# Forgetting attention with weights scaled before they are turned, and an output made in turned form

## What is computed

```python
def forgetting_attention(q, k, v, log_f):
    F = cumsum(log_f, axis=1).transpose(0, 2, 1)
    for blk in range(T // 128):
        logits = einsum('bhqd,bhkd->bhqk', qh[:, :, q0:kend], kh[:, :, :kend])
        logits = logits + F[:, :, q0:kend, None] - F[:, :, None, :kend]
        logits = where(causal, logits, NEG_INF)
        p = softmax(logits, axis=-1)
        outs.append(einsum('bhqk,bhkd->bhqd', p, vh[:, :, :kend]))

h = h + concatenate([ret, fox], axis=-1) @ w_out
```

## Time and profile before

| | us |
|---|---|
| median of 3 runs | 913.65 |
| lowest, highest | 913.23, 914.32 |
| the profiled execution | 913.05 |
| its span, first to last instruction | 911.3 |
| TensorE busy | 898.2 |
| VectorE busy | 586.4 |
| ScalarE busy | 448.1 |
| GpSimd busy | 113.8 |

### The profile page before, as it was taken

The page is one execution under the profiler, slowest core; times in us unless marked ns, Lnnn a source line. Parts: engine busy times, 40 slices in busy tenths (PEclk is TensorE's granted clock), DMA queues, the critical chain, the costliest instruction groups (busy, mean ns, idle before and its releaser), DMA issues.

```text
span 911.3 us, 12621 instructions
## 1 busy us (share of the span) xinstructions
PE 898.2 (99%) x5039; PEld 766.6 (84%) x5039; DVE 586.4 (64%) x834; ACT 448.1 (49%) x632; POOL 113.8 (12%) x83
## 2 busy tenths in 40 slices
PE   9999999999999999999999999999999999999998
PEld 6887887888978999988888889888877888889886
DVE  5378988996686666644456647877765565554542
ACT  6265456854545555533344436645553544444431
POOL 0431225656110000000000002100100000000200
PEclk9999999999999999999999999999999999999999
DMA  8774542334235555555567535524540565554562
GB/s 285 201 247 141 184 139 93 133 112 125 83 104 175 185 185 183 183 188 185 185 203 280 186 94 186 185 93 139 185 138 29 169 203 187 186 173 148 190 216 69
DMA packets 83554, 149.74 MB, mean 164 GB/s; under 512 B 8480, under 2 KB 16208, under 8 KB 83376
## 3 DMA queue, kind: packets, MB, share of 16 engines
q1 hardware_dynamic: 80352, 144.55, 48.3%
q10 hardware_dynamic: 2528, 3.63, 1.1%
q0 software_dynamic: 624, 0.87, 0.8%
HBM read 147.59 MB, written 1.44 MB: 164 GB/s over the span
## 4 chain that ended last, share of the span: by engine, by line
PE 86%; DVE 8%; ACT 2%; DMA 2%; POOL 1%; issue 1%; DVEq 0%; SPq 0%; ACTq 0%; POOLq 0%
PE gemm L494 63%; PE mixbank L980 5%; PE gemm L980 5%; DMA raw<-in_w_in_dram 2%; PE mixbank L677 2%; DVE mix L1942 2%; PE mixbank L555 2%; PE mixbank L652 2%; DVE w_lo L1713 1%; PE mixbank L839 1%; PE mixbank L663 1%; ACT w_hi L1201 1%; POOL mix L2480 1%; PE gemm L566 1%; PE mixbank L1161 1%
## 5 line engine op out<-in xcount | busy, mean ns | idle before, releaser
L1713 DVE TENSOR_TENSOR w_lo<-raw,w_hi 128x2048 fp32r<-128x2048 f32 (+3 forms) x131 | 285.2, 2187 | 187.8 <-ACT w_hi L1201 187.6
L1201 ACT ACTIVATE w_hi<-raw 128x2048 fp32r<-128x2048 f32 (+3 forms) x140 | 255.3, 1833 | 173.2 <-DMA raw<-in_w_in_dram 50.0
L494 PE MATMUL gemm<-w_hi,s_hi 128*128 128x512 f32 (+3 forms) x784 | 208.7, 386 | 0.7 <-issue 0.4
L494 PE MATMUL gemm<-w_lo,s_hi 128*128 128x512 f32 (+3 forms) x784 | 201.7, 377 | 0.1
L494 PE MATMUL gemm<-w_hi,s_lo 128*128 128x512 f32 (+3 forms) x784 | 201.6, 377 | 0.0
L494 PEld LDWEIGHTS gemm<-w_lo,s_hi 128*128 128x128 f32 x784 | 142.7, 188 | 27.5 <-DVE w_lo L1713 0.3
L494 PEld LDWEIGHTS gemm<-w_hi,s_lo 128*128 128x128 f32 x784 | 142.7, 188 | 27.5
L494 PEld LDWEIGHTS gemm<-w_hi,s_hi 128*128 128x128 f32 x784 | 139.7, 188 | 27.4 <-issue 2.8
L2447 POOL TENSOR_TENSOR sm<-sm 128x2 f32<-128x2 f32 (+4 forms) x13 | 22.7, 1750 | 493.0 <-DVE sm L1757 313.2
L2441 POOL TENSOR_TENSOR w_lo<-raw,w_hi 128x2048 fp32r<-128x2048 f32 x9 | 41.3, 4602 | 158.5 <-ACT w_hi L1201 158.5
L1218 ACT ACTIVATE mix<-gemm,sm 128x512 f32<-128x512 f32 (+2 forms) x25 | 16.3, 654 | 60.9 <-PE gemm L494 60.9
(11 more groups left out here) (333 smaller groups left out, 1172.1 us busy)
## 6 DMA issues: line engine op xcount, KB each, us to landing
raw<-in_w_in_dram SPq DMA_DIRECT2D x40, 1024.0 KB, 5.0
raw<-in_w_mlp_up_dram SPq DMA_DIRECT2D x16, 1024.0 KB, 5.3
raw<-in_w_mlp_down_dram SPq DMA_DIRECT2D x16, 1024.0 KB, 5.0
raw<-in_w_gate_dram SPq DMA_DIRECT2D x10, 1024.0 KB, 5.0
raw<-in_w_up_dram SPq DMA_DIRECT2D x10, 1024.0 KB, 5.0
raw<-in_w_down_dram SPq DMA_DIRECT2D x10, 1024.0 KB, 5.0
raw<-in_w_out_dram SPq DMA_DIRECT2D x8, 1024.0 KB, 5.0
raw<-in_w_xkv_dram SPq DMA_DIRECT2D x8, 1024.0 KB, 5.1
```

The lines of the kernel that those rows point to most:

```text
L494: return nc.tensor.matmul(G[b % 2][t][:, 0:width], lhs, rhs, start=kt == 0 and not (low_x or low_w), stop=kt == blk["kt"] - 1 and (low_x i ...
L1201: nc.scalar.activation(w_hi[:, n % SLOTS, 0:kn, 0:width], raw[:, n % SLOTS, 0:kn, 0:width], ACT.Copy)\
L1713: V.tensor_tensor(w_lo[:, s, 0:kn, 0:width], raw[:, s, 0:kn, 0:width], w_hi[:, s, 0:kn, 0:width].bitcast(F32), ALU.subtract)\
```

## The change

- `scaled` on VectorE takes the place of `normed` for the forgetting attention: when the exponentials of a group are there it takes the reciprocal of the sums and multiplies the 128x512 weights in LM2 by it, in place, and then signals `att_norm`. It stands behind `greatest` of the next group and ahead of the copy of its own.
- TensorE's `turned` waits for `att_norm` there instead of `att_exp`.
- `weighed_features` takes the place of `weighed`: values are stationary (64 columns), turned weights move (128 columns). The output has features on partitions; even heads go to partitions 0 to 63, odd heads to 64 to 127 of M[3].
- ScalarE's `fox_out` copies M[3] to a new tile FOXT (in the half of MG2 that is no longer needed), and signals `out_copied`, for which the next `weighed_features` waits.
- The transposes of banks 2 and 3 of MG2 go; `s_hi` and `s_lo` of these are made from FOXT, and B_O2 runs without a break.
- `ret_oc` is renamed `out_copied`; ScalarE counts `turn_pe` by itself.

```diff
-                pe.wait_ge(sem("att_exp"), g + 1)
+                pe.wait_ge(sem("att_norm" if features_out else "att_exp"), g + 1)
...
+                def weighed_features(k):
+                    t, heads = work[k]
+                    g = g0 + k
+                    pe.wait_ge(sem("att_ptc"), g + 1)
+                    if k >= 1:
+                        pe.wait_ge(sem("out_copied"), NT + k)
+                    per = keys_of(work, k) // P
+                    for j, h in enumerate(heads):
+                        o = M[3][64 * (j % 2):64 * (j % 2) + 64, P * (j // 2):P * (j // 2) + P]
+                        for s in range(per):
+                            last = nc.tensor.matmul(o, values(h, s), exps_turned[:, g % 2, (j * per + s) * P:][:, 0:P], start=s == 0, stop=s == per - 1)
+                    last.then_inc(sem("att_out"), 1)
...
-            mm(B_O2, turned=24, quarters=[0])
-            turn(lambda kt, t: MG2[:, t, P * kt:P * kt + P], lambda q: [("att_norm", 12)], banks=range(2, 4))
-            mm(B_O2, turned=24, quarters=[1, 2, 3])
+            mm(B_O2, turned=24)
...
+            def fox_out(k):
+                t, heads = WORK_A[k]
+                n = len(heads) // 2
+                act.wait_ge(sem("att_out"), len(WORK_A) + k + 1)
+                dst = FOXT[:, heads[0] // 2:heads[0] // 2 + n, P * t:P * t + P]
+                nc.scalar.activation(dst, M[3][:, 0:P * n].rearrange("p (a b) -> p a b", a=n), ACT.Copy).then_inc(sem("out_copied"), 1)
...
             for k in attention(WORK_A, lambda t, h: 1.0, lambda g: LM2[:, g % 2], LM2):
                 if k < 2:
                     split(B_KV + 3, k)
...
                 if k >= 4:
                     split(B_O2, k - 4)
+                if k >= 2:
+                    fox_out(k - 2)
+            fox_out(4)
             turn_hi(banks=range(2))
             project(B_KV + 3, KV[:, 0, D + NCOL:2 * D], rs4)
-            turn_hi(banks=range(2, 4))
+            fox_out(5)
+            act.wait_ge(sem("out_copied"), NT + 6)
+            for q in range(2, 4):
+                sig(nc.scalar.activation(s_hi[:, 2 * q:2 * q + 2, :], FOXT[:, 2 * q - 4:2 * q - 2, :], ACT.Copy), "turn_hi")
...
+                def scaled(k):
+                    hs = work[k][1]
+                    g, ns = g0 + k, keys_of(work, k)
+                    a = 4 * (g % 8)
+                    dve.wait_ge(sem("att_exp"), g + 1)
+                    link(V.reciprocal(RSUM[:, a:a + len(hs)], SUMS[:, a:a + len(hs)]))
+                    rows = lm[:, g % 2, :].rearrange("p (a b) -> p a b", b=ns)
+                    V.tensor_tensor(rows, rows, spread(RSUM[:, a:a + len(hs)], 2, ns), ALU.mult).then_inc(sem("att_norm"), 1)
...
                     if 1 <= k <= n:
+                        if dst is None:
+                            scaled(k - 1)
                         turned(k - 1)
-                    if k >= 2:
+                    if k >= 2 and dst is not None:
                         normed(k - 2)
```

More of the change, by code:

```diff
@@ L305, in build @@
         WR = view(ar2, 7184, 3072)
-        MG2 = view(ar2, 10256, NT, D)
+        MG2 = view(ar2, 10256, NT, NCOL)
+        FOXT = view(ar2, 11280, 4, SEQ)
         MEM = view(ar2, 12304, NT, D)
@@ L634, in _, with attention @@
             groups = [0]
-            def attention(work, queries, keys, values, width, exps, exps_turned):
+            def attention(work, queries, keys, values, width, exps, exps_turned, features_out=False):
                 g0, n = groups[0], len(work)
@@ L687, in attention @@
                     if k >= 2:
-                        weighed(k - 2)
+                        (weighed_features if features_out else weighed)(k - 2)
                 groups[0] += n
@@ L1076, in _ @@
             pe.wait_ge(sem("mem_in"), 16)
-            turn(lambda kt, t: MEM[:, t, P * kt:P * kt + P], lambda q: [("ret_oc", q - 1)] if q >= 2 else [])
+            turn(lambda kt, t: MEM[:, t, P * kt:P * kt + P], lambda q: [("out_copied", q - 1)] if q >= 2 else [])
             mm(B_KV, turned=20)
@@ L1099, in _ @@
             for k in attention(WORK_A, lambda h: [qaT[0:66, h, :]], lambda h: [kaT[0:66, h, :]],
-                               lambda h, s: P2F[:, s, FV - 2048 + 64 * h:FV - 2048 + 64 * h + 64], 64, LM2, PTS2):
+                               lambda h, s: P2F[:, s, FV - 2048 + 64 * h:FV - 2048 + 64 * h + 64], 64, LM2, PTS2, features_out=True):
                 if k == 0:
@@ L1222, in turn_hi @@
                 for q in banks:
-                    act.wait_ge(sem("turn_pe"), seen.get("turn_hi", 0) + 1)
+                    seen["turn_pe"] = seen.get("turn_pe", 0) + 1
+                    act.wait_ge(sem("turn_pe"), seen["turn_pe"])
                     if norm is None:
@@ L1562, in _ @@
                 act.wait_ge(sem("ret_o"), t + 1)
-                nc.scalar.activation(MG2[:, t, 0:NCOL], M[2 + t][:, :], ACT.Copy).then_inc(sem("ret_oc"), 1)
+                nc.scalar.activation(MG2[:, t, 0:NCOL], M[2 + t][:, :], ACT.Copy).then_inc(sem("out_copied"), 1)
             turn_hi(NORMS["mem"])
@@ L1874, in _, with attention @@
             groups = [0]
-            def attention(work, scale, width, mask, lm, pts, dst):
+            def attention(work, scale, width, mask, lm, pts, dst=None):
                 g0, n = groups[0], len(work)
@@ L2251, in _ @@
             for t in range(NT):
-                dve.wait_ge(sem("ret_oc"), t + 1)
+                dve.wait_ge(sem("out_copied"), t + 1)
                 ins = V.tensor_reduce(MU[:, 8 * t:8 * t + 8], ret[t], AX_X, ALU.add)
@@ L2301, in _ @@
                 V.tensor_copy(dst, M[e % 4][0:66, :].rearrange("p (a b) -> p a b", a=2)).then_inc(sem("foxT_dve"), 1)
-            for k in attention(WORK_A, 1.0, 64, fox_mask, LM2, PTS2,
-                               lambda t, hs: MG2[:, t, NCOL + 64 * hs[0]:NCOL + 64 * hs[-1] + 64].rearrange("p (a b) -> p a b", b=64)):
+            for k in attention(WORK_A, 1.0, 64, fox_mask, LM2, PTS2):
                 if k in (1, 3):
@@ L2327, in _ @@
             split(B_O2, 1)
-            turn_lo(banks=range(2, 4))
+            for q in range(2, 4):
+                dve.wait_ge(sem("turn_hi"), seen["turn_lo"] + 1)
+                k = slice(2 * q, 2 * q + 2)
+                sig(V.tensor_tensor(s_lo[:, k, :], FOXT[:, 2 * q - 4:2 * q - 2, :], s_hi[:, k, :].bitcast(F32), ALU.subtract), "turn_lo")
             begin(B_O2)
```

## The result

| | before | after |
|---|---|---|
| median (us) | 913.86 | 921.05 |
| lowest, highest | 913.23, 914.32 | 920.91, 922.71 |
| profiled execution, its span | 913.05, 911.3 | 921.02, 919.2 |
| mean granted clock | 1.000 | 0.996 |
| ratio of times, 95% interval | | 1.0084, 1.0072 to 1.0096 |

What follows compares the result with a forecast made beforehand. TensorE, busy 898.2 of 911.3 us, was taken as the bound. Terms 4.65 + 0.2 + 0.3 (group 5) + 0.1 (`weighed`) - 0.95 gave +4.3 us, 917.9 against the median; range 915.2 to 919.7.

Steps and rivals of the forecast that it cites:

- VectorE's backlog: Forgetting attention: VectorE's queued splits, gates and retention delay `scaled`, so TensorE waits; 4.65 us of delay by group 3.
- the third quarter of B_O2: First product reading the copies from FOXT, some 5.5 us after the last `weighed`; copies hidden, or a few tenths if late.
- The rival in which cover holds: TensorE finds group 3 already scaled, by about 611, so the kernel is not slower: 911.5 to 912.7; chance 0.04.
- the sum of 4.3: All priced terms of the change together: 4.3 us slower, 917.9 against the median.
- The falling clock: The 2.6 us stall ahead of group 3 brings TensorE to half speed, losing 2.4 us: 920.3; chance 0.07.
- The delay at group 3: TensorE may transpose group 3 at 615.7 instead of 611.02, delayed 4.65 us by waiting for `scaled`.
- the restart: After a wait, TensorE's four transposes take 0.66 instead of 0.44 us; 0.2 us added after group 3.
- the lower bound of 0.65: Least time of a `weighed` group in us, with good overlap of column halves and cheap entry; upper bound 1.07.
- the prediction's 1.4 us for groups of 0.42: If column tiling halved `weighed` from 0.87 to 0.42 us a group, the sum would be 1.4 us lower.
- The removed transposes: Eight transposes of MG2's last two banks, 0.87 us at 628.62, go with their seams: a gain of 0.95 us.
- wait and restart of group 5: TensorE waits about 0.1 us for `scaled` of group 5, plus 0.2 for the restart: 0.3 us.

Runs made afterwards that it cites:

- e1b_warm3: The changed kernel with three extra 128x512 products on TensorE ahead of the transposes of group 3; 918.01 us, ratio 1.0042.
- e8_stall_only: The kernel before, with TensorE's transposes of group 3 also waiting for VectorE's maxima of group 4; 919.53 us, ratio 1.0057.
- e5: The changed kernel with VectorE's multiply of group k-1 ahead of the maxima of group k instead of behind; 918.31 us, ratio 1.0037.
- e7: The kernel before with only the multiply of the weights moved ahead, products in their old form, eight transposes kept; 923.56 us, ratio 1.0107.
- e8b: The kernel before, transposes of group 3 waiting for the maxima of group 4, plus one unused VectorE multiply ahead of these; 921.13 us, ratio 1.0075.
- the reordered kernel: The changed kernel with VectorE's multiply ahead of the next maxima, retention gates and scaling earlier, B_O2 split later; 912.60 and 912.84 us in two runs.
- e6: The changed kernel with VectorE's multiply ahead of the next maxima, gates in round 0, scaling in round 2, B_O2 split in round 6; 912.60 us, again 912.84.
- e3: The changed kernel with the outputs of all heads on TensorE's lower column half; 919.26 us, ratio 1.0061.
- a2: The changed kernel as it is, measured again on the same chip as other follow-up runs; 920.12 us, ratio 1.0062.
- e1: The changed kernel with six extra 128x512 products on TensorE ahead of the transposes of group 3; 920.47 us, ratio 1.0076.

## Why the prediction was wrong

**What held.** VectorE's backlog was followed row by row, and it came as worked out: waits of 1.07, 0.67, 2.74 and 0.23 against 1.05, 0.5, 2.6 and 0.1; TensorE transposes group 3 at 615.39 in a trace whose stage starts 0.31 us earlier, so at 615.70 by the clock of the trace before, where the prediction had 615.7; the multiply lasts 0.69; the third quarter of B_O2 waits for nothing. The rival in which cover holds was out from the start. With the clock kept up (e1b_warm3) the stage costs 4.23 against the sum of 4.3, with the luck named there.

**What failed: half speed behind the long wait stood in the sum at nothing.** It measured 3.20 us, and without it the stage would have been 4.04 longer instead of 7.24. The falling clock stood there as a rival with its mechanism, its place (the wait ahead of group 3) and a price of 2.4 us, 920.3 in all. It was given a chance of 0.07 and left out of the range, whose upper end of 919.7 the time passed. The reason given against it was that waits of 1.1 and 0.6 us in the cross attention cost no speed. That is true and says nothing about 2.6. The trace of before has no wait of more than 1.6 us, so it left the question open, and the one row that bore on it, the half speed behind the idle start, spoke for it. That the wait does it is shown from both sides: put alone into the kernel before it brings the fall (e8_stall_only), and filled with work in the changed kernel it brings none (e1b_warm3). An unknown that decides 3 us should have had a good part of the chance and the upper end of the range.

**The price of the fall.** 2.4 from the start's products. Measured by the round behind the wait, it took two values: 3.20 in the first profile, 3.23 behind 1.91 us (e5), 3.27 behind 2.53 (e8), 3.17 behind 3.25 (e7) and 3.26 behind 3.79 (e8b), and 1.64 in the second profile of the changed kernel, about half. (The runs with the new `weighed` are set against 4.87, the others against the 4.93 of before.) It isn't bound to the wait's length; what picks the value, the runs don't show.

**Two terms were misread between views.** The delay at group 3 was taken as 615.7 less 611.02, but 611.02 is the chain's time; the start in order of time is 610.86. That is 0.16 of the 0.19 by which 4.65 fell short of 4.84; the rest is rounding. And the restart was priced at 0.2 because four transposes take 0.66 behind a wait in order of time and 0.44 in the chain. In order of time they take 0.60 without a wait as well. From the start of the transposes to `weighed` it is 0.59 behind a wait and 0.53 without: a restart costs 0.06.

**`weighed`.** I priced 0.96 for groups of two heads and 0.75 for four, and took 0.87. It measured 0.59 for both, below the lower bound of 0.65, since the overlap doesn't need the halves to alternate from one product to the next, as I had assumed. Why not, the runs don't show. But the seams grew: from the start of the transposes to that of `weighed` 0.53 instead of 0.43, and from the logits to the products 0.78 instead of 0.73. So a whole round went from 4.93 to 4.83 (606.79 to 611.62 above; 610.86 to 615.79 before) and a group gains 0.1, where the sum had a loss of 0.03. The term was off by 0.13 a group, on the cautious side. (By its own numbers, 4 x 0.45, the prediction's 1.4 us for groups of 0.42 should be 1.8.) That changing between whole and divided array costs time was in those prices as 0.2 and came as 0.15 at the two seams, 0.10 and 0.05; the page "TensorEngine Tiling (Array Packing)" of the Trainium skill (Tiling Modes) says that such a change drains TensorE, and the seams agree in kind. Its factor of up to 2 for two column tiles came as 1.02 to 0.59, or 1.7.

**The removed transposes** were priced at 0.95. From the last `weighed` to the end of the stage the reordered kernel takes 22.53 (625.34 to 647.87), the kernel before 23.57 (624.83 to 648.40) with a `weighed` of 0.81 in place of 0.59: 0.82 for the transposes. The price was 0.13 too high.

| term | forecast | measured |
|---|---|---|
| waits up to the start of `turned` of group 3 | +4.65 | +4.84 |
| its round without the half speed: restart, `weighed` | +0.2 | -0.06 |
| half speed | 0 | +3.20 |
| wait and restart of group 5 | +0.3 | +0.27 |
| last transposes, and `weighed` (+0.1 in the sum) | -0.85 | -1.01 |
| stage | +4.3 | +7.24 |

(The round took 8.07, the filled run's 4.87 and that of before 4.93: the 3.20 and the -0.06. What `weighed` gained in the other rounds is within the lines that it stands in.)

The prediction also named the Trainium skill's page "TensorE: Matmul & The Clock Gate" (Why this matters for your kernels) and its warning of idle gaps between bursts of matmuls. The trace agrees with it in kind: an idle gap in dense work lowered the clock. But the page warns only of gaps longer than this one, and here waits of 1.91 and 2.74 us were enough. The measurement decides.

## What to carry to other kernels

A step that moves ahead of TensorE's work from behind it turns the other engine's backlog into waits, and those can be read off the old trace: follow that engine's queue round by round and set it against TensorE's. A wait inside dense TensorE work can have a second price above some length, here up to 3.3 us. Apart from the kernel's own start, no wait of up to 1.75 us had it in a profile of this study; put any wait near 2 us or more into the range at both prices, and shorten or fill it. When the order of the helping engine is mended, even a change that lost 7 us can keep its small gain.

## What the runs showed of the hardware

**The clock falls on waits of about 2 us, and not surely.** Longest wait of TensorE in the stage, and whether the clock fell behind it. In profiles, where the clock is seen: 0.19 (e6, twice) no; 1.91 (e5) yes; 2.24 (e3) no; 2.53 (e8), 2.74 (after, a2), 3.25 (e7) and 3.79 (e8b) yes; none where products filled the 2.7 us (e1, e1b). By the mean clock of all executions, 0.994 to 0.996 taken as a fall: 1.91 in 7 of 10, 2.24 in 1 of 4, 2.53 in 6 of 6, 2.74 in 8 of 10 (and once more, at 0.998, in a profile), 3.25 and 3.79 in 4 of 4 each. Elsewhere in the kernel waits of 1.11 in the cross attention cost no clock in any profile, nor did one of 1.75 us, for GpSimd, early in the profiled execution of e5:

```profile
69.53 1.31 PE L602 MATMUL mixbank<-cst,mix 128*128 128x128 f32 x10 [1.75 <-POOL mix L2532]
```

That wait is there in every kernel, the one before too, and was 0.31 to 1.75 us long in the profiles; it is one reason why the start of the stage moves. That a wait of 1.91 made the clock fall more often than one of 2.24 suggests that the length alone doesn't decide. What else does, the runs leave open: the executions counted here are too few for it.

**Extra work can make the kernel faster.** Three useless products gained 3.0 us of stage against the first run (58.71 to 55.70), 1.45 against the second; one-sided products that take 0.43 us longer a group gained 1.8 us in the median against the first runs, 0.9 against the second, by shortening the wait.

**Products on two column halves overlap even when those of one half stand together in fours:** 8 instructions in 0.59 us against 1.02 on one half.
